# Two groups of the modulation map moved into layer 0's retention, and the low-rank norm moved into the block of the input projection

## What is computed

```python
def _modulation(cond, w, b):
    m = jax.nn.silu(cond) @ w + b
    return jnp.split(m[:, None, :], 6, axis=-1)
...
    # even layer: one input projection, then latent attention and retention
    q_lat, kv_lat, k_pe, r_q, r_k, r_v, r_g = jnp.split(h @ w_in, EVEN_SPLITS, axis=-1)
    q = (_rmsnorm(q_lat, q_norm) @ w_uq).reshape(b, t, MLA_HEADS, MLA_NOPE_DIM + MLA_ROPE_DIM)
    ckv = _rmsnorm(kv_lat, kv_norm)
    k_pe = _rope_2d(k_pe, *rope)          # latent tokens
...
    o_ret = (_head_norm(o_f) + _head_norm(o_b[:, ::-1])).reshape(b, t, RET_WIDTH) * gn_g * jax.nn.silu(r_g)
    out = jnp.concatenate([o_mla, o_ret], axis=-1) @ w_out
```

## Time and profile before

| | |
|---|---|
| median of 3 executions | 2047.14 us (2039.57 to 2047.60) |
| the profiled execution | 2052.36 us, span 2050.8 us |
| TensorE busy | 1695.3 us (83%) |
| VectorE busy | 672.9 us (33%) |
| ScalarE busy | 342.2 us (17%) |
| GpSimd busy | 317.8 us (15%) |
| DMA | 590.26 MB, mean 288 GB/s |
| clock granted to TensorE, mean | 0.888 |

### The profile page before, as it was taken

The page is one execution under the profiler, slowest core; times in us unless marked ns, Lnnn a source line. Parts: engine busy times, 40 slices in busy tenths (PEclk is TensorE's granted clock), DMA queues, the critical chain, the costliest instruction groups (busy, mean ns, idle before and its releaser), DMA issues. The chain is left out here.

```text
span 2050.8 us, 19679 instructions
## 1 busy us (share of the span) xinstructions
PE 1695.3 (83%) x7044; PEld 875.0 (43%) x7044; DVE 672.9 (33%) x1278; ACT 342.2 (17%) x772; POOL 317.8 (15%) x248
## 2 busy tenths in 40 slices
PE   3995889677999959989896769959999978898876
PEld 1553477344444423333332657545444323333322
DVE  3212346585323101111116747474322111111117
ACT  2110440001111101111111325101111111111120
POOL 0001001030111112332210400211211113211110
PEclk8997775777999989999998879968999989999997
DMA  9895010318899999999978110337999999999965
GB/s 391 341 345 198 11 42 6 129 43 334 316 409 414 404 418 400 410 395 390 404 281 350 43 52 1 129 136 289 357 398 417 394 398 415 404 386 381 382 266 234
DMA packets 113572, 590.26 MB, mean 288 GB/s; under 512 B 23272, under 2 KB 25320, under 8 KB 55744
## 3 DMA queue, kind: packets, MB, share of 16 engines
q1 hardware_dynamic: 88640, 535.39, 65.0%
q0 software_dynamic: 24256, 50.54, 6.4%
q10 hardware_dynamic: 576, 3.03, 0.4%
HBM read 576.14 MB, written 48.40 MB: 305 GB/s over the span
## 5 line engine op out<-in xcount | busy, mean ns | idle before, releaser
L2179 PE MATMUL bank<-weights,scratch 128*64 128x512 f32 x448 | 221.0, 651 | 91.7 <-DMA scratch<-in_moe_w_up 45.9
L2284 DVE TENSOR_TENSOR scratch<-scratch,bank 128x256 f32<-128x256 f32 x88 | 53.9, 613 | 677.6 <-ACT scratch L2253 648.8
L2180 PE MATMUL bank<-scratch 128*64 128x512 f32 x480 | 231.5, 639 | 0.0
L2179 PEld LDWEIGHTS bank<-weights,scratch 128*64 128x64 f32 x448 | 64.8, 150 | 237.3 <-issue 237.3
L2253 ACT ACTIVATE scratch<-bank 128x256 f32<-128x256 f32 x88 | 33.8, 384 | 712.6 <-PE bank L2180 434.4
L2179 PE MATMUL bank<-scratch 128*64 128x512 f32 x288 | 132.0, 613 | 17.3 <-DMA scratch<-in_moe_w_up 17.3
L2185 PE MATMUL bank<-weights,scratch 128*128 128x512 f32 x320 | 141.9, 596 | 2.8 <-ACT scratch L2248 1.7
L2180 PE MATMUL bank<-weights,scratch 128*64 128x512 f32 x256 | 122.2, 633 | 0.0
L1985 POOL DMA_INDIRECT y_rows<-hP,y_idx x42 | 43.3, 1031 | 463.9 <-DVE hP L2289 396.0
L2185 PE MATMUL bank<-scratch 128*128 128x512 f32 x256 | 112.9, 594 | 0.0
L2212 PE MATMUL bank<-scratch 128*64 128x512 f32 x240 | 109.4, 598 | 0.0
(11 more groups left out here) (340 smaller groups left out, 2749.8 us busy)
## 6 DMA issues: line engine op xcount, KB each, us to landing
weights<-in_moe_w_gate SPq DMA_DIRECT2D x64, 1024.0 KB, 13.7
weights<-in_moe_w_up SPq DMA_DIRECT2D x64, 1024.0 KB, 15.6
weights<-in_moe_w_down SPq DMA_DIRECT2D x64, 1024.0 KB, 19.1
scratch<-in_moe_w_gate SPq DMA_DIRECT2D x64, 1024.0 KB, 12.2
scratch<-in_moe_w_up SPq DMA_DIRECT2D x64, 1024.0 KB, 20.9
scratch<-in_moe_w_down SPq DMA_DIRECT2D x64, 1024.0 KB, 18.2
weights<-in_w_mod SPq DMA_DIRECT2D x10, 2048.0 KB, 9.1
wmod_more<-in_w_mod SPq DMA_DIRECT2D x10, 2048.0 KB
```

The costliest lines, as they stand in the source:

```text
L2179: nc.tensor.matmul(out[0:HALF, :], x[:, 0:HALF], w0[:, kk], start=(kk == 0), stop=(kk == KT - 1))
L2180: m = nc.tensor.matmul(out[HALF:P, :], x[:, HALF:P], w1[:, kk], start=(kk == 0), stop=(kk == KT - 1))
L2284: nc.vector.tensor_tensor(B.h[b % 2].rearrange("p (j q) -> p q j", j=2), B.ex[b % 2].rearrange("p (q j) -> p q j", j=2), k.ps[2 + b % 2][: ...
```

## The change

Four things:

1. The modulation groups 4 and 5 (the last two) are no longer multiplied in the projection block. They go into retention, as sixteen halves of a piece (1 MB each, four matmuls): one behind the products of each step from i = 9 to i = 24, from three slots in the work memory. The bias, the adding and the writing of the rows move along, and their DMAs go from POOL's queue to SP's.
2. In the projection block 12 pieces are left: one ahead of the first tile, and one behind each tile from b = 1 to b = 11.
3. `stage_mla_norm` is gone. Its work is done inside the projection block: squares on ACT behind chunk 0's copies, the power on POOL, the normalising and the rotary part on DVE behind chunk 1's copies; the three MLA weights are loaded behind the last piece, into the ring.
4. In the first stage the first piece for the projection block is issued between w_in's first two chunks, instead of behind them.

The views of the norm's buffers move (`mla_norm_views`, `mla_views`). The core of the diff:

```diff
+MOD_HALVES = KT
+LATE_GROUPS = (DEPTH * 6 * D // MOD_COLS - 2, DEPTH * 6 * D // MOD_COLS - 1)
...
+def mod_half(k, n):
+
+    group, kk = divmod(n, MOD_HALVES)
+    layer, c = mod_group(LATE_GROUPS[group])
+    return k.io["w_mod"][layer].rearrange("(p k) n -> p k n", k=KT)[:, kk, c:c + MOD_COLS]
+
+
+def pe_mod_half(k, n, bank, w):
+    kk = n % MOD_HALVES
+    for j in range(4):
+        m = k.nc.tensor.matmul(k.ps[bank][32 * j:32 * j + 32, :], k.cond[:, kk, :], w[:, 512 * j:512 * (j + 1)], start=(kk == 0), stop=(kk == MOD_HALVES - 1))
...
-            first_chunks(k, w, 2)(sp)
-            k.load_ahead(sp, 2, piece_view(k.ring[:, 8192:12288]), mod_piece(k, MOD_PIECES))
+            for i, (c, n) in enumerate(chunks_of(w.shape[1])[:2]):
+                k.load_ahead(sp, i, ring_slot(k, i)[:, :, 0:n], w.rearrange("(k p) n -> p k n", p=P)[:, :, c:c + n])
+                if i == 0:
+                    k.load_ahead(sp, 2, piece_view(k.ring[:, 8192:12288]), mod_piece(k, MOD_PIECES))
...
-    groups = range(1, DEPTH * 6 * D // MOD_COLS)
-    pieces = range(MOD_PIECES, MOD_PIECES * (groups[-1] + 1))
-    assert len(groups) == N
+    groups = range(1, LATE_GROUPS[0])
+    pieces = range(MOD_PIECES, MOD_PIECES * LATE_GROUPS[0])
+    assert len(groups) < N
...
+            def chunk(j):
+                c, n = chunks[j + 2]
+                sp.wait_ge(s_wl, 2 * (j + 1))
+                sp.dma_start(ring_slot(k, j % 2)[:, :, 0:n], w.rearrange("(k p) n -> p k n", p=P)[:, :, c:c + n]).then_inc(s_w[j % 2], 16)
+
+            def mla_norm_loads():
+                sp.wait_ge(s_xl, TILES)
+                sp.dma_start(m["qg"], io["mla_q_norm"][e:e + 1, :].to_broadcast([P, Q_RANK])).then_inc(s_l, 16)
+                sp.dma_start(m["kvg"], io["mla_kv_norm"][e:e + 1, :].to_broadcast([P, KV_RANK])).then_inc(s_l, 16)
+
+                sp.dma_start(m["ckv"][:, 3, :], io["cache_mla_ckv"][0, e]).then_inc(s_l, 16)
+                sp.dma_start(m["kpe"][:, 3, NOPE:QK], io["cache_mla_kpe"][0, e]).then_inc(s_l, 16)
+
+            def mla_weights():
+                sp.wait_ge(s_wh, 2 * (N - 1))
+                sp.wait_ge(s_wl, 2 * (N - 1))
+                k.load_ahead(sp, 3, m["wuq"], io["mla_w_uq"][e].rearrange("(k p) n -> p k n", p=P))
+                k.load_ahead(sp, 4, m["wuk"], io["mla_w_uk"][e])
+                k.load_ahead(sp, 4, m["wuv"], io["mla_w_uv"][e])
+
+            def mla_outputs():
+                sp.wait_ge(s_n, 1)
+                sp.dma_start(io["new_mla_ckv"][0, e], m["ckv"][:, 0, :]).then_inc(s_new, 16)
+                sp.dma_start(io["new_mla_kpe"][0, e], z[:, 0, Z_PE:Z_RQ]).then_inc(s_new, 16)
+
             for n in pieces:
-                i = n - MOD_PIECES
-                if i % MOD_PIECES == 2 and i // MOD_PIECES + 2 < N:
-                    j = i // MOD_PIECES
-                    c, m = chunks[j + 2]
-                    sp.wait_ge(s_wl, 2 * (j + 1))
-                    sp.dma_start(ring_slot(k, j % 2)[:, :, 0:m], w.rearrange("(k p) n -> p k n", p=P)[:, :, c:c + m]).then_inc(s_w[j % 2], 16)
+                if n % MOD_PIECES == 2:
+                    chunk(n // MOD_PIECES - 1)
                 piece(n)
+                if n == pieces[1]:
+                    mla_norm_loads()
+            mla_outputs()
+            mla_weights()
+            sp.wait_ge(s_new, 32)
...
+            def rstd():
+                pool.wait_ge(s_ms, 2)
+                nc.gpsimd.tensor_tensor(m["rstd"], m["ss"], m["half"], ALU.pow).then_inc(s_p, 1)
...
-                    upto = (b + 1) * len(pieces) // (N * TILES)
+                    mm.then_inc(s_mm, 1)
+                    upto = max(done, min(b + 1, len(pieces)))
...
+            def squares():
+                act.wait_ge(s_v, 1)
+                act.wait_ge(s_a, 2)
+                act.wait_ge(s_xl, TILES)
+                for t in range(TILES):
+                    nc.scalar.activation(m["junk"][:, 0:Q_RANK], z[:, t, 0:Z_KV], ACT.Square, accum_out=m["ss"][:, t:t + 1]).then_inc(s_sq, 1)
+                    act.wait_ge(s_sq, 2 * t + 1)
+                    nc.scalar.activation(m["junk"][:, 0:KV_RANK], z[:, t, Z_KV:Z_PE], ACT.Square, accum_out=m["ss"][:, 3 + t:4 + t]).then_inc(s_sq, 1)
+                    act.wait_ge(s_sq, 2 * t + 2)
...
+                if i == 0:
+                    squares()
...
+            def mean_squares():
+                dve.wait_ge(s_sq, 2 * TILES)
+                nc.vector.tensor_scalar(m["ss"][:, 0:3], m["ss"][:, 0:3], 1.0 / Q_RANK, RMS_EPS, ALU.mult, ALU.add).then_inc(s_ms, 1)
+                nc.vector.tensor_scalar(m["ss"][:, 3:6], m["ss"][:, 3:6], 1.0 / KV_RANK, RMS_EPS, ALU.mult, ALU.add).then_inc(s_ms, 1)
+
+            def normed():
+                dve.wait_ge(s_p, 1)
+                dve.wait_ge(s_l, 64)
+                for t in range(TILES):
+                    st.mark(nc.vector.scalar_tensor_tensor(m["qn"][:, t, :], z[:, t, 0:Z_KV], m["rstd"][:, t:t + 1], m["qg"], ALU.mult, ALU.mult))
+                    st.mark(nc.vector.scalar_tensor_tensor(m["ckv"][:, t, :], z[:, t, Z_KV:Z_PE], m["rstd"][:, 3 + t:4 + t], m["kvg"], ALU.mult, ALU.mult))
+                st.mark(nc.vector.tensor_copy(m["kpe"][:, 0, NOPE:QK], z[:, 0, Z_PE:Z_RQ]))
+                st.wait()
+                nc.vector.memset(m["tmp"][:, 0:1], 0.0).then_inc(s_n, 1)
+                dve.wait_ge(s_n, 1)
+                for t in (1, 2):
+                    x = z[:, t, Z_PE:Z_RQ].rearrange("p (h a b f) -> p h a b f", h=1, a=2, b=2)
+                    rope(nc, st, k, C_ROPE_E, t - 1, x, m["tmp"], 1, ROPE // 4)
+                    st.then(nc.vector.tensor_copy(m["kpe"][:, t, NOPE:QK], z[:, t, Z_PE:Z_RQ]))
...
-                if i:
+                if i == 0:
+                    mean_squares()
+                if i == 1:
+                    normed()
+                if 1 <= i <= len(groups):
                     mod_rows(i)
-            mod_rows(N)
...
-            k.arrived(pe, 0)
+            k.arrived(pe, 3)
...
+    late = [cut(MOD_COLS), cut(MOD_COLS), k.s[:, 15104:15104 + MOD_COLS]]
...
+            def half(n):
+                if n >= 3:
+                    sp.wait_ge(s_mod, n - 2)
+                sp.dma_start(late[n % 3], mod_half(k, n)).then_inc(s_l[n % 3], 16)
+
+            def bias_in(g):
+                layer, c = mod_group(LATE_GROUPS[g])
+                for r in range(2):
+                    sp.dma_start(bias[r:P:32, :], mod_strips(io["b_mod"][layer], c)).then_inc(s_b, 16)
+
+            def rows_out(g):
+                layer, c = mod_group(LATE_GROUPS[g])
+                sp.wait_ge(s_row, g + 1)
+                for r in range(2):
+                    sp.dma_start(mod_strips(k.mod_d[layer, r], c), rows[r:P:32, :]).then_inc(s_out, 16)
+
+            bias_in(0)
+            for n in range(3):
+                half(n)
             ahead(sp)
             sp.wait_ge(s_ssa, 2)
             for d, n in enumerate(("new_ret_fwd", "new_ret_bwd")):
                 sp.dma_start(io[n][0, e].rearrange("h d n -> d h n"), S1[:, d, :].rearrange("p (h n) -> p h n", h=RH)).then_inc(s_store, 16)
+            for n in range(3, HALVES):
+                half(n)
+                if n == MOD_HALVES + 4:
+                    rows_out(0)
+                    bias_in(1)
+            rows_out(1)
+            sp.wait_ge(s_out, 64)
...
+            def mod(n):
+                if n == 0:
+                    pe.wait_ge(s_ssa, 2)
+                pe.wait_ge(s_l[n % 3], 16 * (n // 3 + 1))
+                pe_mod_half(k, n, 2 + n // MOD_HALVES, late[n % 3]).then_inc(s_mod, 1)
+
             for i in range(TILES * RH + 1):
                 if i < TILES * RH:
                     attend(i)
@@ -1292,6 +1401,8 @@
                     values(i - 1)
                 if i == RH - 2:
                     states()
+                if i > RH:
+                    mod(i - RH - 1)
...
+            def mod_rows(g):
+                dve.wait_ge(s_mod, MOD_HALVES * (g + 1))
+                dve.wait_ge(s_b, 32 * (g + 1))
+                if g:
+                    dve.wait_ge(s_out, 32 * g)
+                nc.vector.tensor_tensor(rows, k.ps[2 + g][:], bias, ALU.add).then_inc(s_row, 1)
...
                     prepare(h)
                 else:
                     norm(t - 1, h)
+                if i == 2 * RH + 1:
+                    mod_rows(0)
             for part in range(8):
                 norm(TILES - 1, part)
+                if part == 3:
+                    mod_rows(1)
```

More of the change, by code:

```diff
@@ L589, in stage_project, with stage_project_beside_mod @@
     k.take_upper()
-def stage_project_beside_mod(k, w, n_cols, out):
+def stage_project_beside_mod(k, w, e):
     nc, io = k.nc, k.io
-    chunks = chunks_of(n_cols)
+    chunks = chunks_of(EVEN_IN)
+    m = mla_norm_views(k)
+    z = k.z[:].rearrange("p (t n) -> p t n", t=TILES)
     N = len(chunks)
@@ L623, in stage_project_beside_mod @@
         s_mod, s_row = sems(nc, ctx, "piece_used rows_ready")
```

(49 more changed lines are left out.)

84 lines of the change are left out of this document (6 added, 78 removed).

## The result

The changed kernel took 2022.63 us (median of 4 executions, 2021.39 to 2025.59), the kernel before 2047.37 (4 executions, 2039.57 to 2052.49). The medians differ by 24.7 us. The ratio is 0.9885, 95% interval 0.9862 to 0.9909. Forecast were 2021 us, and faster by more than 0.5%. Medians leave out the one execution in this text, of `e9_threes_from_step_8`, that fell into a slow state (2511 us, at a mean granted clock of 0.64).

A forecast was written before the change was run, and what follows sets the result against it. TensorE was taken to set the pace in the projection block and in retention, there at clock 0.50. Terms -50.7 - 3.0 + 26.8 + 0.7 = -26.2 us took the median 2047.1 to 2021 us, range 1990 to 2033.

The forecast's parts named there:

- Term 1: Start of the projection block: first piece issued earlier lands at about 42.3 us, first tile starts 5.2 us earlier.
- Term 2: Projection block with eight pieces fewer: key stage starts at 150.8 instead of 201.57 us, a gain of 50.7 us.
- No wait above 1 us behind the first: Projection block, a sign to look for: TensorE waits for no piece above 1 us after the first piece.
- Term 3: Norm beside the projection: its work fits behind the chunks' copies at cost zero, at most the old stage's 12.2 us.
- Term 4: Key stage: TensorE arrives from dense work and keeps clock 1.00, gaining 3 us of a possible 4.
- Term 5: Retention: fifteen halves on the path at 1.79 us each lose 26.8 us; added rows in DVE's tail 0.7 us.
- The attention: Attention between key stage and retention: no change forecast, some 5 us of margin for its clock changes.
- A: Retention, the forecast itself: the clock stays at 0.50, total 2021 us; chance 0.62.
- B: Retention: the halves lift the clock to 1.00 and the 26.8 us loss vanishes, total 1994 us; chance 0.20.
- C: Projection block stays bound by DMA, or the norm is not hidden: +10 us, total 2031 us; chance 0.12.
- D: Retention: each half's slot waits for its load to land, steps of 7.6 us, total 2058 us; chance 0.03.

The follow-up runs named there:

- e9_threes_from_step_8: Against `e8_piece_first_threes`, groups of three retention halves start one step earlier, behind steps 8, 11, 14, 17, 20, the last half behind 23; 1998.05 us, ratio 0.9781.
- e6_piece_first: Changed kernel, but SP issues the projection block's third piece ahead of chunk 2 and the norm's four small loads; 2017.04 us, ratio 0.9857.
- e8_piece_first_threes: `e6_piece_first`, with the retention halves also multiplied three at a time behind every third step from step 9; 2003.59 us, ratio 0.9798.
- e3_two_halves: Changed kernel with fourteen of the sixteen retention halves left out, loads and products; 1996.96 us, ratio 0.9777.

## Why the prediction was right, and where it was off

**Term 1** (5.2 us) was too small where it was looked for and too large where it counted. The piece landed at 41.04 and not at 42.3, the first tile came 6.5 us earlier; by the run that undoes it alone, the edit brings the keys 3.1 us and the median 3.8. The text followed the chunk that was put behind the piece, and not the third piece, whose own place on SP became the bound.

**Term 2** (keys at 150.8) held to 1.7 us: 152.46. The intervals of 7.56 us came as in the earlier trace rows. What was missing is the third piece, 3.9 us: 2.27 of waiting, 1.35 for a piece at the slow clock, 0.27 in the products behind it. The earlier start gave 1.3 of them back, and the first two tiles, the last three and the change of stage some 0.3 each. "No wait above 1 us behind the first" failed at this one place.

**Term 3** (the norm at cost zero) is the step that failed. Its work on the engines did disappear: the squares lie at 66.6 to 69.6 us on ScalarE and the normalising at 95.6 to 100.7 on VectorE, and no wait of TensorE comes from either; in `e6_piece_first` the pieces keep their 7.56 us over both. But the prediction named the four small loads "ahead of chunk 2, which is wanted at 90", and stopped there. The third piece stands behind that chunk on the same queue and is wanted at 64. The projection ends 3.5 us later with the norm in it than without.

**Term 4** (3.0 us, at most 4) measured 26.24 - 22.60 = 3.64. The clock was at 1.00 when the block's products ended, and the stretch of transposes and products from 152.50 to 161.50 us shows 1.00. The rule of the Trainium skill ("TensorE: Matmul & The Clock Gate", section on PE-mode transpose) by which the term would have been zero did not decide here.

**Term 5** (26.8 us, and 0.7 for VectorE) was mis-sized. A half costs 5.05 - 3.00 = 2.05 us, not 1.79: that is as much as the upper bound per half (2.03, one load of a stationary operand more), but what it is made of was not isolated: 271.66 - 269.80 = 1.86 us for the half itself and 0.19 on the rest of the step (269.80 - 266.61 = 3.19 instead of 3.00). Retention grew by 118.29 - 88.07 = 30.2 us. Up to the scores of the last step (361.04 before, 327.62 after) fourteen halves give 28.4 of them. The stretch behind, to the transposes of the output (385.14 and 353.49), gives 1.8. Of these, 0.6 are the added rows, forecast at 0.7: VectorE's tail lasts from 334.88 instead of from 367.13, 18.6 us instead of 18.0. The other 1.2 are the fifteenth half. The sixteenth costs nothing, as forecast.

**The attention** was given 0, give or take 5 us, and became 9.1 shorter in the profiled execution. Its instructions are the same. Before, from 227.80 to 288.90 us (columns as above):

```profile
227.80:288.90 61.10, 49.61 (x240) 38.95 (x241) 17.24 (x45) 36.04 (x116) 0.00 (x0) 0.72 0.05 10
```

TensorE is busy 49.61 us in place of 39.85, at a clock of 0.72 in place of 0.90. In all twelve profiles this stage takes 51.5 to 61.1 us. `e6_piece_first` and `e8_piece_first_threes` come to it within 0.4 us of each other by the same instructions, and take 57.80 and 51.57. So this term is luck as far as these traces go, and the margin of 5 us for it was too small. How much of it is in the medians is open, as each kernel has one trace.

**The rivals.** A held: 0.50 from 258 us to the end of retention. The sum was -26.2; the span shows -30.9 and the medians -24.7. It came out right partly by luck, because errors went both ways: in the span, the keys' start is 1.6 us behind the forecast and retention 2.7, the rest 0.7; the key stage is 0.6 ahead, and the attention 9.1. Without the attention's 9.1 the span would have shrunk by 21.8 us, 4.4 less than forecast. B is false for this order and true in part for another: three halves in a row lift the clock, and take 18.4 of retention's added 30.2 us away. What was said against it, that two thirds of each step stay as they are, fits what came, though no run isolated it; that the order of the halves was free was not seen. B's price was too high besides: a step of a latent tile at 1.00 takes 1.73 us without its half, not 2.0. The Trainium skill's rule (same page, section "Why this matters for your kernels") that a TensorE kept continuously busy gets the full clock is again not borne out: 69.60 of 69.60 us busy at 0.50. C's half on the norm was the better guess on the direction, at 3.5 us instead of 10. DMA did not bound the block as a whole, at 292 GB/s, but it did for a moment: during the wait for the third piece the DMA share is 1.00, at 418 GB/s. D is out: without the loads retention takes as long.

One reading of the prediction is off without consequence: by the earlier trace rows the clock is reduced in slices 3 to 9 (counted from 0), so up to 513 us and not to 461.

## What to carry to other kernels

When work is moved under a cover, price its loads at their place in the queue: ask which transfer stands next but one behind them, and when that one is wanted. Where TensorE sits at the slow clock though it never waits, the order of its matmuls is a variable of its own: gathering the wide ones behind every third step instead of one behind each shortened retention by 18 us at equal work, and the median by 15. And compare kernels that alter values by stages, since data can move the total by more than the edit.

## What was not expected of the chip

- Order alone moves the granted clock. Sixteen groups of eight recorded matmuls of 512 columns, one behind twelve narrow ones each, leave it at 0.50; by twos it rose once, for some 7 us; by threes its mean is 0.73. What exactly lifts it was not isolated.
- Identical instructions differ by almost ten us from kernel to kernel: 51.5 to 61.1 us for the attention, at a clock of 0.90 in the changed kernel and of 0.72 in the one before. What decides where the clock changes was not found.
- A late load can cost more than the wait. TensorE stood still for 2.27 us and lost 3.9: behind the wait the piece took 3.28 us instead of 1.92. It need not: in `e3_two_halves` the wait was 3.29 us, and the piece took 1.92.
- Data can move layer 1 from 754 to 791 us. With other modulation values one expert had more tokens than its first pass takes, and the branch for it lasted 37.8 us.
